# A chunk loop of four passes with six chunks each, instead of eight with three

## What is computed

```python
def _rwkv7_step(state, inputs):
    r, decay, kk, a, k, v = inputs
    sa = jnp.einsum("bhvk,bhk->bhv", state, kk)
    state = (state * decay[:, :, None, :]
             - sa[..., None] * (kk * a)[:, :, None, :]
             + v[..., None] * k[:, :, None, :])
    y = jnp.einsum("bhvk,bhk->bhv", state, r)
    return state, y
...
    _, y = lax.scan(_rwkv7_step, state0, xs)
```

## Time and profile before

| | |
|---|---|
| median of 3 runs | 4993.88 us (4987.54 to 4996.01) |
| the profiled execution | 4985.64 us |
| its span, first to last instruction | 4983.9 us |
| TensorE busy, share of the span | 4465.6 us, 90% |
| VectorE | 2340.3 us, 47% |
| ScalarE | 1670.7 us, 34% |
| GpSimd | 763.0 us, 15% |
| first transpose of chunk 0, and of chunk 6 (the loop's start) | at 3352.4 and 3532.9 us |
| first transpose of chunk 30 (behind the loop) | at 4294.2 us |

### The profile page before, as it was taken

How to read it: one execution, slowest core, us unless ns; L and a number is a source line. 1 busy time by engine, 2 the same in 40 slices (tenths; PEclk the granted TensorE clock), 3 DMA queues, 4 the chain that set the end, 5 groups by cost and what they waited for, 6 DMA issues and landing times. The chain is left out here.

```text
span 4983.9 us, 106350 instructions
## 1 busy us (share of the span) xinstructions
PE 4465.6 (90%) x41048; PEld 3571.6 (72%) x41048; DVE 2340.3 (47%) x2853; ACT 1670.7 (34%) x3166; POOL 763.0 (15%) x596
## 2 busy tenths in 40 slices
PE   5999999978999999878889888888888888889979
PEld 5888888866888877645555555557777777768867
DVE  4444444434444444366667766663444434442222
ACT  3222222222222222145556555553333333331111
POOL 2111111111111111000000000003434334411012
PEclk9999999989999999989999999999999999999989
DMA  2444455552555555533332323311222222244333
GB/s 69 109 108 108 108 108 108 109 123 92 117 111 107 115 116 106 123 66 70 82 81 52 76 51 83 82 51 47 73 69 70 68 59 70 75 153 143 115 122 126
DMA packets 484768, 463.36 MB, mean 93 GB/s; under 512 B 275648, under 2 KB 377536, under 8 KB 478288
## 3 DMA queue, kind: packets, MB, share of 16 engines
q1 hardware_dynamic: 466752, 423.08, 36.4%
q10 hardware_dynamic: 17680, 35.66, 2.4%
HBM read 297.09 MB, written 161.55 MB: 92 GB/s over the span
## 5 line engine op out<-in xcount | busy, mean ns | idle before, releaser
L1480 POOL TENSOR_TENSOR off<-NT,tri 128x512 f32<-128x512 f32 x198 | 245.9, 1271 | 1905.2 <-ACT NT L1403 1905.2
L1060 ACT ACTIVATE keep<-z 128x512 f32<-128x512 f32 (+3 forms) x704 | 346.0, 507 | 471.6 <-PE z L972 325.2
L1108 DVE TENSOR_TENSOR_SCAN kept<-keep,kept 128x512 f32<-128x512 f32 (+1 forms) x448 | 436.9, 975 | 126.0 <-ACT keep L1060 89.6
L971 PE MATMUL z<-k_high,q_parts 128*128 128x512 f32 (+3 forms) x704 | 317.1, 451 | 136.6 <-ACT keep L1060 108.9
L982 PE MATMUL turned<-t_identity,kept 128*128 128x128 f32 (+1 forms) x2432 | 380.0, 279 | 35.3 <-DVE kept L1108 34.9
L1105 DVE TENSOR_TENSOR_SCAN kept<-keep,hidden 128x512 f32<-128x512 f32 (+3 forms) x256 | 286.7, 1125 | 249.2 <-ACT keep L1060 235.7
L1010 PE MATMUL acc<-w,dv 128*64 128x512 f32 (+4 forms) x1280 | 377.1, 555 | 23.4 <-DMA dv_diag<-scr_v_edge 23.4
L1068 ACT COPY w<-turned 128x512 f32<-128x512 f32 (+4 forms) x704 | 363.0, 527 | 85.3 <-PE turned L982 72.3
L971 PEld LDWEIGHTS z<-k_high,q_parts 128*128 128x128 f32 x704 | 142.1, 202 | 332.1 <-ACT keep L1060 228.1
L982 PEld LDWEIGHTS turned<-t_identity,kept 128*128 128x128 f32 (+1 forms) x2432 | 285.1, 137 | 112.4 <-DVE kept L1108 37.9
L1457 DVE TENSOR_TENSOR X<-even,eye 128x256 f32<-128x256 f32 x330 | 140.0, 424 | 439.0 <-PE even L1349 437.8
(11 more groups left out here) (462 smaller groups left out, 10274.8 us busy)
## 6 DMA issues: line engine op xcount, KB each, us to landing
w_raw0A<-in_w_main SPq DMA_DIRECT2D x42, 512.0 KB
w_raw0B<-in_w_main SPq DMA_DIRECT2D x42, 512.0 KB, 4.0
w_raw1A<-in_w_main SPq DMA_DIRECT2D x41, 512.0 KB, 4.1
w_raw1B<-in_w_main SPq DMA_DIRECT2D x41, 512.0 KB, 4.0
KB<-scr_kb SPq DMA_DIRECT2D x33, 512.0 KB, 3.4
AR<-scr_ar SPq DMA_DIRECT2D x33, 512.0 KB, 4.9
k_high<-scr_k_hi SPq DMA_DIRECT2D x32, 516.0 KB, 11.5
k_low<-scr_k_lo SPq DMA_DIRECT2D x32, 516.0 KB, 13.4
```

The lines of the kernel that those rows point to most:

```text
L971: pe.matmul(out, queries, k_high[u][:, k0:k0 + size], start=True, stop=False)
L1060: act.activation(keep[num % KB][:, 0:size], z[num % ZB][:, 0:size], ACT.Sigmoid, scale=-DH ** -0.5).then_inc(keep_done, 1)
L1108: dve.tensor_tensor_scan(dst, data, data, kept[g % 2][:, end:end + 1], ALU.mult, ALU.bypass).then_inc(scanned, 1)
L1480: pool.tensor_tensor(out, a, b, op).then_inc(s[name], 1)
```

## The change

In `walk` the loop has `(NCH - PEELED) // 6` = 4 passes in place of `(NCH - PEELED) // 3 - 1` = 8, and its body calls `body` six times in place of three. The 24 chunks are the same ones, n from 6 to 29. The buffer is b % 3 and the turn is (PEELED + b) // 3 + 2i, which give every chunk the buffer and the wait values that it had. The change holds on all five engines, since all of them use `walk`.

```diff
             for n in range(PEELED):
                 body(n, n % 3, n // 3)
-            with eng.Fori(0, (NCH - PEELED) // 3 - 1) as i:
-                for b in range(3):
-                    body(PEELED + b + 3 * i, b, PEELED // 3 + i)
+            with eng.Fori(0, (NCH - PEELED) // 6) as i:
+                for b in range(6):
+                    body(PEELED + b + 6 * i, b % 3, (PEELED + b) // 3 + 2 * i)
             for n in range(NCH - 3, NCH + 3):
                 body(n, n % 3, n // 3)
```

## The result

The changed kernel takes 5003.58 us in the median of 22 runs (4990.71 to 5021.67), the kernel before in 22 runs beside them 4992.89 us (4980.26 to 5006.19). The ratio is 1.0021, with a 95% interval of 1.0012 to 1.0030: it is slower by 0.2%, 10.7 us between the medians, where 25 us less had been forecast. The profiled execution has a span of 5004.4 us, against 4983.9.

The account below looks back on a forecast made before the run. TensorE, busy 90% of the span, was taken to bound the kernel. Standstill 15.1 us plus slow clock 10.1 us, other terms 0, made some 25 us off the 4993.88 us median: 4969 us, range 4958 to 4984.

Parts of the forecast that it names:

- What bounds the loop, and what an edge costs: Chunk loop: TensorE sets the pace and idles 26.5 us at seven edges, refetching its long body; a slower clock follows.
- the other engines' bodies are free: Doubled loop bodies on ScalarE, VectorE and the other engines: taken to cost 0.
- the rival in which one of them fetches again: Loop edges: ScalarE or VectorE must fetch its longer body, giving back up to 12 us; 4981 us, chance 0.08.
- (a): TensorE's standstill at the chunk loop's edges: four edges fewer at 3.79 us each save 15.1 us.
- (c): Straight entries to chunks 9, 15, 21 and 27: nothing new comes late once the standstill is gone, 0 us.
- (d): TensorE's stops at fetched-block borders in straight code: 0 in the sum, 6 us allowed to either side.
- a sign of being wrong: Chunk loop: stops at block borders adding up to more in the second halves than in the first.
- The third rival: Second halves of the long passes: worse block borders lose 32.5 us, giving 5001 us; chance 0.03.
- (b): TensorE's lower clock behind an edge: 2.53 us a body, four bodies lose it, saving 10.1 us (0 to 11.8).
- The first rival: Chunk loop: only the standstill goes, since border stops lower the clock too; 4979 us, chance 0.13.

Follow-up runs that it names:

- others alone long: Kernel before with six chunks a pass on the four other engines, TensorE keeping three: ratio 1.0001 (0.9993 to 1.0010).
- The runs with cut loads: Kernel before and changed kernel, each with SyncE's loads in the loop cut to an eighth: spans of 4950.2 and 4947.4 us.
- the second pair: Changed kernel and kernel before, each run again unaltered for a second trace: 5006.42 us, ratio 1.0035, and 4986.31 us, ratio 1.0001.
- other borders: Changed kernel with head_slot 192 set for TensorE's loop, which moves the borders of its instruction blocks: ratio 1.0018 (1.0006 to 1.0030).

## Why the prediction was wrong

**What bounds the loop, and what an edge costs** was right. TensorE sets the pace, 3.4 to 4.0 us go at each edge for a body of this length, the clock falls behind it (to 0.50 for 3.41 us from 3626.28), and the other engines' bodies are free (others alone long: 1.0001). Their longer bodies were held: in the changed kernel the next instruction follows a taken branch within 0.3 us on ScalarE and on VectorE, and L1399 starts 2.0 us or less behind the transposes. So the rival in which one of them fetches again didn't occur. Its working had a slip that bore on nothing: 9.1 us behind 3624.6 VectorE would have been back at 3633.7, 2.3 us late and not about on time. That the attention loop's body is still there and the chunk loop's is fetched anew was my reading of the lengths, and the DMA records of before show it: from 2265.4 to 3358.2 us no packet of q8 starts, while the attention loop comes round seven times with 1418 matmuls and weight loads a pass (its branches are at 2284.9 to 3341.1), and in the chunk loop, with 4285 a pass, 19 start on each of the first seven passes and 18 on the last. At which length between the two a body no longer stays was not tried.

**(a), the standstill:** 15.1 us forecast, 26.5 - 10.9 = 15.6 measured. **(c)** held at 0: no transpose at the four straight entries waits.

**(d) is the step that failed.** I saw the stops at block borders, took them for a property of single addresses, and put 0 into the sum with 6 us to either side. They cost 14.5 us more than before. Within the chunks of the second halves they add up to 32.1 us, within those of the first to 14.2, which I had named as a sign of being wrong. What I left out of the working is that instruction blocks and loads share the 16 DMA engines, though the profile had both: the instruction queue's packets in the page, counted in shares of those engines (0.3%), and a stop in the midst of a group, 11 us into the chunk, soon behind SyncE's issues. The runs with cut loads show that this makes most of the stops in either body. They don't show it for the 14.5 us by which the long body has more, since 12.1 of them were left with an eighth of the data; why straight code of this length meets more stops stays open. The third rival, worse borders, had the place of the loss and nearly its price: it decides from 2.1 us a chunk, and the second halves ran 6 / 3 = 2.0 us a chunk slower than assumed. It had a chance of 0.03 because six straight chunks "show nothing of it"; but they are samples of a few positions of the borders, and the twelve new chunks had others. That its 5001 us lies close to the measured 5003.58 is luck: in the traces the stage took as long as before, and what was lost in the whole was lost ahead of it.

**(b), the clock:** 10.1 us forecast, none seen in the first pair of traces (44 us at the lower level in both); in the second pair it is 34 us against 44. The changed kernel has four straight entries at 1.00, as said, but 0.98 and 0.96 over the second halves. The rows before already showed a fall behind a border stop of 1.86 us (0.50 for 3.41 us from 3670.66), and stops of 2.8 us are nearer to an edge's 3.8 than to those. The first rival, only the standstill goes, had this right, though not its total. The 2.4 GHz that were put beside a clock of 1.00, and the 1.2 beside its other level, 0.50, are estimates, at one column a cycle. At 0.50 the projection's matmuls of 512 columns start every 427 ns (L409 to L411, around 1138 us), which is 1.2 columns a ns. At 1.00 they start every 227 ns, and those of 384 columns every 173: 128 columns in 53 ns, 2.4 a ns.

**The projection** is a term that the sum lacked. That the rest of the kernel stays as it is was taken for granted; it was true of the instructions executed and not of the time: 15 us ahead of the stage, the mean of the six traces with the long body (3370.7) less that of the eight with the short one, no unreached matmuls on TensorE (3355.5). Together with the stage, which took 756.2 us in the mean of three traces with the long body (borders and loads as they are in it) against 761.8 in the mean of the eight traces with the short body, its loads in one go and no hint, that is 15.2 - 5.6 = 9.6 us, beside the 10.7 and 20.5 of the two pairs of medians. The delay is clear of the traces' scatter. The 5.6 us are not: the eight lie between 755.1 and 768.3 us, and with other borders the long body took 766.5. So the loss in the whole is made by this term, as far as the traces tell, while whether the stage by itself gained 0.1% or nothing is not shown. The forecast was wrong in the stage by (d) already; that the result is slower and not merely unchanged is due to a term that I had not thought of.

## What to carry to other kernels

Here a loop whose body TensorE fetched anew on every pass (18 or 19 packets of 16 KB each time, where the attention loop's seven later passes drew none) paid 3.3 to 4.0 us at each edge, but it also paid at the borders of the blocks in which its instructions arrive, most of it when loads filled the DMA engines at that moment (31.7 us of such stops with whole loads, 1.5 with an eighth of them). So look for idle time in the midst of a group of instructions that waits for nothing, and for the instruction queue's packets just ahead of it. Unrolling helped most together with loads that are issued in small parts over the body: twelve chunks a pass alone brought 0.2%, spread loads alone 0.1%, both together 0.8%, and spread loads with no loop 1.1%. And a change of program length can delay stages that it doesn't touch, here by 15 us where 25 were hoped for, so an unreached stretch of code of the same length is a control worth a run.

## What was not expected of the hardware

- Instructions that are never reached delay other stages: with 4490 of them on TensorE chunk 0 starts some 15 us later and the median is 0.21% up; with as many on VectorE chunk 0 is in its usual range and the ratio is 0.9995, with 1 in its interval.
- A hint that names the branch's target ahead takes 1.6 of 3.9 us off the branch, and lengthens the stops within the chunks by more in all (10.3 us less, 13.1 more).
- TensorE's short stops at block borders are nearly absent in one case: 1.5 us in 24 chunks of the short body with cut loads, where 31.7 were with full ones.
